# Squares of the layer norm behind attention: summed by GpSimd instead of by eight TensorE matmuls

## The reference, cut to what matters

```
for i in range(DEPTH):
    x = layer_norm(alpha * x + 0.5 * swiglu(x, ...), ...)
    y = token_mix(x, ...)                       # attention heads and HGRN2, times W_out
    x = layer_norm(alpha * x + y, ln_g[i, 1], ln_b[i, 1])      # the norm of this change
    x = layer_norm(alpha * x + 0.5 * swiglu(x, ...), ...)
    x = x + sigmoid(x @ ple_gate_w[i] + ple_gate_b[i]) * (p[i] @ ple_w[i])
```

## Time and profile before

| what | us |
|---|---|
| median of 3 runs | 2261.65 |
| lowest and highest | 2260.66, 2262.77 |
| span of the profiled execution (first to last instruction) | 2258.9 |
| PE busy in it | 2217.0 |
| DVE, ACT, POOL busy in it | 1135.0, 871.7, 155.2 |

### The profile page before, as it was taken

The page is one execution under the profiler, slowest core; times in us unless marked ns, Lnnn a source line. Parts: engine busy times, 40 slices in busy tenths (PEclk is TensorE's granted clock), DMA queues, the critical chain, the costliest instruction groups (busy, mean ns, idle before and its releaser), DMA issues.

```text
span 2258.9 us, 29068 instructions
## 1 busy us (share of the span) xinstructions
PE 2217.0 (98%) x11971; PEld 1787.4 (79%) x11971; DVE 1135.0 (50%) x1802; ACT 871.7 (39%) x1325; POOL 155.2 (7%) x136
## 2 busy tenths in 40 slices
PE   8999999999999999999999999999999999999998
PEld 6888887877667888888888888878776778888887
DVE  4333344888757333343643333448887663333444
ACT  3232222655755232222532222245466452232233
POOL 0000021211001000011000000212200000000210
PEclk9999999999999999999999999999999999999999
DMA  5333333322213333323333333323322233333222
GB/s 155 102 95 95 95 94 89 89 65 76 80 39 89 108 98 93 107 86 101 90 94 95 101 93 93 93 73 97 76 66 67 66 93 94 103 94 105 88 84 70
DMA packets 383700, 202.66 MB, mean 90 GB/s; under 512 B 17360, under 2 KB 380752, under 8 KB 383568
## 3 DMA queue, kind: packets, MB, share of 16 engines
q1 hardware_dynamic: 383568, 200.80, 31.0%
HBM read 198.68 MB, written 2.10 MB: 89 GB/s over the span
## 4 chain that ended last, share of the span: by engine, by line
PE 84%; DVE 8%; ACT 4%; issue 2%; DMA 1%; SPq 0%; DVEq 0%; ACTq 0%
PE banks L246 24%; PE banks L248 24%; PE banks L247 24%; PE banks L273 2%; PE banks L274 2%; PE banks L279 2%; DVE lev L1030 2%; DVE att L1066 1%; PE banks L1307 1%; DVE w_lo L238 1%; PE banks L1248 1%; PE banks L1294 1%; ACT w_hi L232 1%; ACT lev L916 1%; PE banks L1250 1%
## 5 line engine op out<-in xcount | busy, mean ns | idle before, releaser
L238 DVE TENSOR_TENSOR w_lo<-w_raw,w_hi 128x1024 fp32r<-128x1024 f32 (+2 forms) x378 | 456.6, 1212 | 861.9 <-ACT w_hi L232 861.6
L246 PE MATMUL banks<-xhi,w_hi 128*128 128x512 f32 x1888 | 744.4, 394 | 1.4 <-DVE proj L1002 1.1
L248 PE MATMUL banks<-xhi,w_lo 128*128 128x512 f32 x1888 | 736.2, 390 | 0.0
L247 PE MATMUL banks<-xlo,w_hi 128*128 128x512 f32 x1888 | 735.7, 390 | 0.0
L232 ACT ACTIVATE w_hi<-w_raw 128x1024 fp32r<-128x1024 f32 (+2 forms) x378 | 377.3, 1000 | 848.5 <-PE banks L248 823.5
L246 PEld LDWEIGHTS banks<-xhi,w_hi 128*128 128x128 f32 x1888 | 356.2, 189 | 77.5 <-issue 2.6
L248 PEld LDWEIGHTS banks<-xhi,w_lo 128*128 128x128 f32 x1888 | 354.5, 188 | 74.6
L247 PEld LDWEIGHTS banks<-xlo,w_hi 128*128 128x128 f32 x1888 | 355.0, 188 | 73.8 <-issue 1.9
L246 PE MATMUL banks<-hhi,w_hi 128*128 128x512 f32 x704 | 277.4, 394 | 0.0
L248 PE MATMUL banks<-hhi,w_lo 128*128 128x512 f32 x704 | 274.2, 389 | 0.0
L247 PE MATMUL banks<-hlo,w_hi 128*128 128x512 f32 x704 | 274.1, 389 | 0.0
(11 more groups left out here) (249 smaller groups left out, 1956.2 us busy)
## 6 DMA issues: line engine op xcount, KB each, us to landing
w_raw<-in_ffn_w_gu_dram SPq DMA_DIRECT2D x176, 512.0 KB, 3.9
w_raw<-in_ffn_w_down_dram SPq DMA_DIRECT2D x64, 512.0 KB, 3.6
w_raw<-in_w_in_dram SPq DMA_DIRECT2D x48, 512.0 KB, 4.1
w_raw<-in_ffn_w_down_dram SPq DMA_DIRECT2D x32, 384.0 KB, 3.2
w_raw<-in_w_out_dram SPq DMA_DIRECT2D x32, 256.0 KB, 2.9
w_raw<-in_ple_gate_w_dram SPq DMA_DIRECT2D x16, 512.0 KB, 4.1
w_raw<-in_cmp_k_w_dram SPq DMA_DIRECT2D x16, 256.0 KB, 3.0
w_raw<-in_cmp_v_w_dram SPq DMA_DIRECT2D x16, 256.0 KB, 3.7
```

The costliest lines, as they stand in the source:

```text
L238: dve.tensor_tensor(part_view(wlo, n), raw_view(split_at[n]).rearrange("p k n -> p (k n)"), part_view(whi, n), ALU.subtract).then_inc(sems ...
L246: pe.matmul(bank, w_hi, x_hi, start=first, stop=False)
L247: pe.matmul(bank, w_hi, x_lo, start=False, stop=False)
L248: return pe.matmul(bank, w_lo, x_hi, start=False, stop=last)
```

## The change

POOL now adds up squares too. Behind each addition to `xsum` it waits for ACT's square of the same tile and adds it to a new tile `sqsum_m`; the first addition takes squares 0 and 1 and raises `sq_used` by two, the later ones by one. The squares get four buffers (parts of `lev`) instead of two. PE no longer multiplies squares 0 to 6: it waits for POOL's last addition and multiplies the sum once, between the matmuls of `xsum` and of the last tile, and after them the last square.

```diff
         def squares_act(act, i, sq, tiles):
             for j in tiles:
                 act.wait_ge(*upto("y_ok", i, j + 1))
-                if j >= 2:
-                    act.wait_ge(*upto("sq_used", i, j - 1))
-                act.activation(sq[j % 2], xT[:, j, :], ACT.Square).then_inc(sems["squared"], 1)
+                if j >= len(sq):
+                    act.wait_ge(*upto("sq_used", i, j - len(sq) + 1))
+                act.activation(sq[j % len(sq)], xT[:, j, :], ACT.Square).then_inc(sems["squared"], 1)
...
-        sq_m = [lev[:, 0, :], lev[:, 1, :]]
+        sq_m = [lev[:, k, :] for k in range(4)]
+        sqsum_m = lev[:, 4, :]
...
-            def squared(j):
-                pe.wait_ge(*upto("squared", i_norm, j + 1))
-                return pe.matmul(ps[:, 7, :], mean_w[:], sq_m[j % 2], start=(j == 0), stop=(j == DT - 1))
-
...
             att_piece(5, None, ATT_BANK[5])
-            for j in range(2):
-                squared(j).then_inc(sems["sq_used"], 1)
             pe.wait_ge(*upto("y_raw", i_norm, 1))
             att_piece(6, None, ATT_BANK[6])
-            for j in range(2, 4):
-                squared(j).then_inc(sems["sq_used"], 1)
             pe.wait_ge(*upto("y_raw", i_norm, 2))
             att_piece(7, None, ATT_BANK[7])
-            for j in range(4, DT - 1):
-                squared(j).then_inc(sems["sq_used"], 1)
             pe.wait_ge(*upto("acc", i_norm, DT - 2))
             pe.matmul(ps[:, 6, :], mean_w[:], xsum[:], start=True, stop=False)
+            pe.wait_ge(*upto("sq_used", i_norm, DT - 1))
+            pe.matmul(ps[:, 7, :], mean_w[:], sqsum_m, start=True, stop=False)
             pe.wait_ge(*upto("y_ok", i_norm, DT))
             pe.matmul(ps[:, 6, :], mean_w[:], xT[:, DT - 1, :], start=False, stop=True).then_inc(sems["mean_mm"], 1)
-            squared(DT - 1).then_inc(sems["sq_mm"], 1)
+            pe.wait_ge(*upto("squared", i_norm, DT))
+            pe.matmul(ps[:, 7, :], mean_w[:], sq_m[(DT - 1) % len(sq_m)], start=False, stop=True).then_inc(sems["sq_mm"], 1)
             keep_on(pe, 32)
...
                 pool.tensor_tensor(xsum[:], xT[:, 0, :] if j == 1 else xsum[:], xT[:, j, :], ALU.add).then_inc(sems["acc"], 1)
+                pool.wait_ge(*upto("squared", i, j + 1))
+                if j > 1:
+                    pool.wait_ge(*upto("sq_used", i, j))
+                pool.tensor_tensor(sqsum_m, sq_m[0] if j == 1 else sqsum_m, sq_m[j % len(sq_m)],
+                                   ALU.add).then_inc(sems["sq_used"], 2 if j == 1 else 1)
```

## The result

The changed kernel takes 2277.2 us (median of 4 runs, 2276.78 to 2278.56), the kernel before in the same comparison 2261.16. That is 16.0 us more, ratio 1.0071 with a 95% interval of 1.0057 to 1.0085. The prediction said 2279.7, range 2272.5 to 2284.5. The profiled execution has a span of 2275.6 us and a time of 2277.45.

A forecast was written before the change was run, and what follows sets the result against it. PE is busy 98% of the span, but a chain through DVE sets the norm's end. Two layers of +6.9 (wait for POOL) and +2.1 (clock) give +18.0 us: span 2276.9, median 2279.7, range 2272.5 to 2284.5.

The forecast's parts named there:

- PE spectator before, and the removed work worth 0: End of the norm: a chain through DVE sets it, PE has waits, so PE's removed squares gain 0.
- The price of an addition and the exclusion with DVE: POOL's queue: 1.29 us an addition alone, more beside DVE since they exclude each other; squares' sum complete at 707.5.
- The new wait of PE at full clock, +6.9 a layer: PE waits for POOL's sums until 707.5; line 341 starts at 710.5 instead of 703.59, +6.9 us a layer.
- The clock, +2.1 a layer: After PE's 12.8 us pause the norm's matmuls run partly at half clock: bounds 0 and 3.0, taken +2.1 us a layer.
- Downstream nothing: From line 341 on nothing changes; the 5.9 us to the first FFN matmul stay.
- The 1.3 us: Norm's matmuls behind PE's pause: clock cost per layer if full clock returns after 3.4 us of work.
- The sign given for line 341: Timeline of layer 0: line 341 at 712.6 rather than 703.59.
- The low end of the range: Whole kernel: 2272.5 us, the clock staying up and each POOL addition 0.1 us shorter, put at 1.5 us a layer less.
- the high end: Whole kernel: 2284.5 us, from 6.9 + 3.0 + 1.5 a layer, 1.5 for half-clock filler or additions at 1.56.
- B: Rival on PE's wait in the norm: same wait, clock stays at 1.0, 2275.5 us; chance 0.15.
- C: Rival on POOL's queue: additions much quicker when unbroken, 2265.9 us, up to 2272; chance 0.08.
- D: Rival on the norm's end: faster, PE's squares behind the last piece being late, 2254.8 us; chance 0.02.

The follow-up runs named there:

- e6: The changed kernel without POOL's additions of squares (squares 0 to 5 left out of the variance), with 31 filler matmuls in PE's pause: 2261.48 us against 2261.58 before.
- e5: The kernel before with four square buffers, DVE adding the last tile before splitting the third FFN weight, ACT splitting it before square 6: 2259.17 us, ratio 0.9990.
- e3: The changed kernel with 62 filler matmuls (11.9 us) in PE's wait for POOL: 2277.72 us against 2261.33 before, ratio 1.0072.
- e10: The changed kernel run again, unaltered, in one comparison with its version with filler in PE's wait: 2279.42 us against 2262.18 before, ratio 1.0074.
- e1: The changed kernel without POOL's six additions of squares; PE multiplies square 6 in place of their sum, squares 0 to 5 left out: 2266.07 us, ratio 1.0020.
- e2: The kernel before with four buffers for the squares in place of two, all eight squares through PE: 2261.31 us against 2261.33 before, ratio 1.0000.
- e9: Second run of the changed kernel with 62 filler matmuls in PE's wait for POOL: 2275.91 us against 2262.18 before, ratio 1.0060.
- e7: The kernel before with four square buffers, PE's seven early squares behind the last piece, two FFN weight splits behind the last tile's addition: 2259.12 us, ratio 0.9987.

## Why the prediction was right, step by step

*PE spectator before, and the removed work worth 0.* Right for the work itself: e6 leaves POOL's squares out, holds the clock and takes as long as the kernel before. The hiding work that the prediction named, DVE's queue, is the late link (e5).

*The price of an addition and the exclusion with DVE.* Right. It had 20.34 us from the first start to the last end, it was 19.94. The last four are 0.24 us of the difference: priced at their duration of 1.29, they start every 1.22 us. The first eight are 0.12, 15.02 us where 15.14 was forecast. One reading was loose: line 238 at 699.64 starts behind POOL's end at 699.54, so its 1.23 us are wholly, not mostly, without POOL.

*The new wait of PE at full clock, +6.9 a layer.* It was +6.5 and +6.4: 19.94 us on POOL, then the 2.99 us that e3 shows at full clock, less 16.43 and 16.54.

*The clock, +2.1 a layer.* The mechanism was right, the size too large: 4.26 and 4.88 us behind POOL's end against 2.99, so +1.3 and +1.9. In e10 it is 4.20 and 5.62, +1.2 and +2.6. The term is not a constant, as it depends on when in the four matmuls the clock is back. The 1.3 us stood for a clock that is back after 3.4 us of PE's work, as at the kernel's start. Here it was back 3.3 and 4.6 us behind the start of the `xsum` matmul, in e10 3.2 and 6.0. The prediction had the middle of 1.3 and 3.0, and the measured four average 1.75.

*Downstream nothing.* Right: 5.9 us from line 341 to line 273 in both.

The sum is 6.5 + 6.4 + 1.3 + 1.9 = 16.1 us, and the medians differ by 16.0. Of the 2.0 us by which 18.0 was too much, 0.9 are POOL's and 1.0 the clock's. Both errors point the same way, so none hid another. The sign given for line 341 was 712.6, and it came at 712.11. That is closer by luck: POOL started 0.75 us later than before, and counted from its first start line 341 followed after 24.2 us where 25.4 was forecast. The low end of the range has a slip of its own: twelve additions 0.1 us shorter are 1.2 us a layer, not 1.5, so by its own reason it is 2273.1. And the 1.5 us in the high end is more than the 1.1 that four additions 0.27 longer give. Neither bound was touched.

What the prediction missed is how the two causes hang together. It charged the clock to the long wait for POOL alone. e1 shows that the removal of PE's squares brings the clock down with no addition moved at all: 4.7 us of the 16 are there before POOL has a single square to add. The rest, 11.3 us, comes with the additions. The split depends on the order in which the causes are put in: with the clock held in e3 the norms lose 13.3 us to POOL alone, and the clock adds 2.8 to that. e1 is thus also the case of a POOL that is never late, and it still loses.

Rivals: B (clock stays up) is out, seen in the granted clock. C (POOL much quicker unbroken) holds for 0.07 us an addition and no more. D (PE's squares are the late link) is out by e2, where ACT's wait for them is gone, and by e6, where most of them are.

Open: how the falls of the clock elsewhere in layer 1 depend on what is changed here. They were seen in single executions (e3, e9) and not pursued. Open too is what sets the moment at which the clock falls and comes back inside the norm; the cost per layer ran from 1.2 to 2.6 us in one and the same kernel.

## What to carry to other kernels

Before moving work from a full engine to an idle one, ask whose queue ends last at that place: here PE was 98% busy and the twelve matmuls taken from it gained nothing, while POOL had 155 us of work in 2259 and no room for six additions in the 12 us where they had to be. POOL additions beside a DVE that reads two SBUF tiles cost both engines; here they took 1.7 to 2.3 us and not their 1.3 alone. And work that only fills a wait of PE may be what keeps its clock up: if it is removed, look at the granted clock first. What did help here was order, by 2.4 us of 2261 (e5, e7): the tile that all others wait for goes ahead of a weight split that the FFN, 10 us later, is the first to need.

## What the runs showed of the hardware that was not expected

- A PE pause of 6.0 us in layer 0 and 6.2 in layer 1, between dense matmuls before and after, brought the granted clock to 0.5 in e1; from the first of the four matmuls behind it to line 341 it took 6.5 us in layer 0, and 3.8 in e6 with the clock up.
- Back-to-back POOL additions of 128x512 float32 with no DVE beside them start every 1.22 us though each is shown as 1.26 long.
